# RWKV stage of a hybrid diffusion step, reordered around its serial chains, with the key norm moved into the stage before

## The reference

```python
kkf = heads(kc * k_k)                                    # keys of the RWKV branch
kk = kkf * lax.rsqrt(jnp.sum(kkf * kkf, axis=-1) + 1e-12)     # the key norm
decay = jnp.exp(-jnp.exp(-jax.nn.softplus(-(w0[d] + tanh(wlr) @ w2[d])) - 0.5))
a = jax.nn.sigmoid(a0[d] + alr @ a2[d])
kd = kc * (1 + (a - 1) * k_a)
# per token, per direction, per head:
sa = einsum('bhij,bhj->bhi', s, -kk)
s = s * wt + sa * (kk * a) + vt * kt
y = einsum('bhij,bhj->bhi', s, rt)
```

## Time and profile before

| | us |
|---|---|
| median of 3 runs (2185.05 to 2187.41) | 2186.7 |
| the profiled execution's own time | 2176.87 |
| its span | 2175.1 |
| PE busy, share of the span | 1938.8, 89% |
| stage 3, layer 0 | 455.6 to 761.1 |
| stage 3, layer 1 | 1528.5 to 1800.1 |

### The profile page before, as it was taken

How to read it: one execution, slowest core, us unless ns; L and a number is a source line. 1 busy time by engine, 2 the same in 40 slices (tenths; PEclk the granted TensorE clock), 3 DMA queues, 4 the chain that set the end, 5 groups by cost and what they waited for, 6 DMA issues and landing times.

```text
span 2175.1 us, 35742 instructions
## 1 busy us (share of the span) xinstructions
PE 1938.8 (89%) x15251; PEld 1568.5 (72%) x15251; DVE 1025.5 (47%) x1715; ACT 817.8 (38%) x1310; POOL 296.4 (14%) x550
## 2 busy tenths in 40 slices
PE   6899898967888888999989999989768888899998
PEld 2799445644565588999989975556446668899998
DVE  0326425847463464433333444286656655434332
ACT  1533544253332345333234344333523344533321
POOL 2000000007455000000000000000275520000000
PEclk9999999987989999999999999999889999999999
DMA  7443334301303143443443432433010203344442
GB/s 263 135 120 107 103 97 128 115 25 40 98 2 99 45 164 97 118 134 110 122 133 100 127 99 80 141 102 117 6 44 18 60 7 116 97 136 117 118 120 83
DMA packets 267782, 214.32 MB, mean 99 GB/s; under 512 B 7210, under 2 KB 259401, under 8 KB 267369
## 3 DMA queue, kind: packets, MB, share of 16 engines
q1 hardware_dynamic: 264640, 204.43, 31.1%
q0 software_dynamic: 2736, 7.54, 1.1%
q10 hardware_dynamic: 248, 0.07, 0.0%
HBM read 209.13 MB, written 2.88 MB: 97 GB/s over the span
## 4 chain that ended last, share of the span: by engine, by line
PE 74%; DVE 9%; ACT 8%; POOL 3%; issue 3%; DMA 1%; PEld 1%; PEldq 1%; DVEq 0%; ACTq 0%; POOLq 0%
PE bank L554 11%; PE bank L555 11%; PE bank L556 11%; PE bank L610 8%; PE bank L605 7%; PE bank L930 3%; PE bank L1110 3%; PE bank L1109 3%; PE bank L1108 3%; PE bank L616 3%; PE bank L506 2%; POOL cst L1191 2%; PE bank L794 2%; POOL lora L1189 2%; ACT h L1255 1%
## 5 line engine op out<-in xcount | busy, mean ns | idle before, releaser
L556 PE MATMUL bank<-scr_rounded 128*128 128x384 f32 (+1 forms) x1312 | 443.0, 338 | 0.0
L554 PE MATMUL bank<-scr_rounded 128*128 128x384 f32 x672 | 231.8, 345 | 36.0 <-DVE scr_rounded L1676 34.2
L610 PE MATMUL bank<-h,ring 128*128 128x384 f32 x640 | 240.6, 522 | 20.2 <-ACT gtmp L1238 14.2
L556 PEld LDWEIGHTS bank<-scr_rounded 128*128 128x128 f32 (+1 forms) x1312 | 248.8, 190 | 1.0
L555 PE MATMUL bank<-scr_rounded 128*128 128x384 f32 x672 | 229.5, 342 | 0.0
L1671 DVE TENSOR_TENSOR scr_rounded<-ring,scr_rounded 128x2048 fp32r<-128x2048 f32 (+1 forms) x64 | 136.0, 2126 | 175.9 <-ACT scr_rounded L1246 175.1
L554 PE MATMUL bank<-scr_rounded,gate_rounded 128*128 128x384 f32 (+1 forms) x640 | 214.0, 334 | 4.4 <-DVE scr_rounded L1671 4.4
L555 PE MATMUL bank<-scr_rounded,gate_rounded 128*128 128x384 f32 (+1 forms) x640 | 213.8, 334 | 0.0
L610 PEld LDWEIGHTS bank<-h,ring 128*128 128x128 f32 x640 | 121.9, 200 | 107.6 <-issue 40.0
L605 PE MATMUL bank<-ring,scond 128*2 128x256 f32 x768 | 177.1, 383 | 23.8 <-ACT modrow L1225 8.2
L1671 DVE TENSOR_TENSOR scr_rounded<-ring,gate_rounded 128x2048 fp32r<-128x2048 f32 (+3 forms) x64 | 130.2, 2034 | 104.8 <-ACT gate_rounded L1246 104.3
(11 more groups left out here) (368 smaller groups left out, 3218.1 us busy)
## 6 DMA issues: line engine op xcount, KB each, us to landing
ring<-in_w_in_dram SPq DMA_DIRECT2D x56, 1024.0 KB, 5.3
ring<-in_w_ada_dram SPq DMA_DIRECT2D x48, 1024.0 KB, 5.2
ring<-in_w_ffn_in_dram SPq DMA_DIRECT2D x88, 512.0 KB, 5.1
ring<-in_w_ffn_out_dram SPq DMA_DIRECT2D x32, 704.0 KB, 4.6
ring<-in_w_out_dram SPq DMA_DIRECT2D x8, 1024.0 KB, 5.2
ring<-in_w_po_a_dram SPq DMA_DIRECT2D x4, 1024.0 KB, 6.3
ring<-in_w_po_b_dram SPq DMA_DIRECT2D x4, 1024.0 KB, 5.4
ring<-in_w_po_c_dram SPq DMA_DIRECT2D x4, 1024.0 KB, 5.2
```

Source lines behind the costliest of these rows:

```text
L554: pe.matmul(o, w_hi[:, k, :], right[0][k], start=k == 0, stop=False)
L556: ins = pe.matmul(o, w_lo[:, k, :], right[0][k], start=False, stop=k == nk - 1)
L610: ins = pe.matmul(b[:, 0:T], w[:, k, 128 * (j % 2):128 * (j % 2) + 128], h[:, k, :], start=k == 0, stop=k == KD - 1)
```

## The change

- The squares of the keys and their sums move from stage 3 into stage 2, with their own buffers `kkn`. `unit_keys` for all pairs comes first on DVE in stage 3. `loras(0)` moves ahead of the barrier.
- `reads` (RT) goes right behind W, ahead of FT. The second half of a group's terms is split (`keys`, `terms`), and the two groups of the next pair go between the evictions of the state chain. Before, they stood behind `factors`.
- `grams(n + 1)` goes ahead of `turned(n)`. `ee` gets a third buffer.
- `FILLS` becomes a list for each layer, with more places, and `side_plan(2)` puts its two gates last.

```diff
-        FILLS = ((2, 8, 2, 0), (2, 2, 4, 0), (2, 2, 4, 0), (2, 2, 0, 4))
+        FILLS = ((4, 4, 4, 4, 6, 0, 2, 4, 2, 1, 1, 1, 0, 0, 1, 2, 1, 1, 1, 0, 0, 1, 2, 1, 1, 1, 2, 2, 2, 2, 2, 1, 1, 1),
+                 (4, 4, 4, 4, 4, 0, 2, 4, 0, 1, 1, 1, 0, 0, 1, 1, 1, 1, 1, 0, 0, 1, 1, 1, 1, 1, 2, 2, 2, 0, 0, 1, 1, 1))
...
-                return po[0:4] + ada[0:4] + po[4:8] + [gate_of(1, 0), ada[4], gate_of(1, 1)] + ada[5:8]
+                return po[0:4] + ada[0:4] + po[4:8] + ada[4:8] + [gate_of(1, 0), gate_of(1, 1)]
...
-                fill(4)
+                for hp in range(4):
+                    pe.wait_ge(S["rw_kksq"], told("rw_kksq", l, hp + 1))
+                    pe.wait_ge(*room())
+                    b = item("A", "kkms", l, hp)
+                    pe.matmul(b[:, 0:T], blocks, kkn[hp], start=True, stop=True).then_inc(psum_ready, 1)
+                fill(3)
...
-                    fill(2)
+                    fill(2 if n < 12 else 1)
...
@@ PE, stage 3 @@
+                fill(next(steps))
                 loras(2)
                 grams(0)
+                fill(next(steps))
+                loras(3)
+                fill(next(steps))
                 for n in range(5):
                     if n:
                         merges(n - 1)
                         transitions(n - 1)
+                        fill(next(steps))
                         scan_step(n - 1, 0)
-                        reads(n - 1)
+                        if n < 3:
+                            loras(2 * n + 3)
                         scan_step(n - 1, 1)
-                        fill(1)
+                        fill(next(steps))
                         scan_step(n - 1, 2)
-                        fill(1)
+                        fill(next(steps))
                         outputs(n - 1)
...
@@ ACT, stage 2 @@
+                for hp in range(4):
+                    A(kkn[hp], pc[:, 4 + hp, :], ACT.Square, scale=P(l, "k_k", hp)).then_inc(*tells("rw_kksq"))
                 act.wait_ge(S["gla_abs"], told("gla_abs", l, 1))
...
@@ ACT, stage 3 @@
+                decays(2)
                 for n in range(5):
...
@@ DVE, stage 3 @@
                     if n:
                         inverses(n - 1)
+                        reads(n - 1)
                     if n < 3:
-                        logs(2 * n + 2)
+                        keys(2 * n + 2)
                     if n:
                         transitions(n - 1)
+                    if n < 3:
+                        terms(2 * n + 2)
+                    if n:
                         scan_step(n - 1, 0)
-                        reads(n - 1)
                         scan_step(n - 1, 1)
+                    if n < 3:
+                        logs(2 * n + 3)
+                    if n:
                         scan_step(n - 1, 2)
+                    if n < 3:
+                        keys(2 * n + 3)
+                        terms(2 * n + 3)
                     if n < 4:
                         factors(n)
                         if n < 3:
-                            terms(2 * n + 2)
-                            logs(2 * n + 3)
-                            terms(2 * n + 3)
+                            grams(n + 1)
+                        if n < 2:
+                            logs(2 * n + 4)
                         turned(n)
```

More of the change, by code:

```diff
@@ L830, in loras @@
                         pe.matmul(b[:, 0:T], lora[hr[d], w, 128 * hp:128 * hp + 128], pc[hr[d], src, :], start=True, stop=True).then_inc(psum_ready, 1)
+                pe.wait_ge(S["rw_lora"], told("rw_lora", l, 1))
+                loras(0)
+                finish(l, 2)
+                barrier(pe, "pe", l, 2)
+                side[0] = side_steps(side_plan(l, 3))
                 def grams(n):
@@ L1394, in _ @@
                 A(lg, lg, ACT.Ln, bias=1.0).then_inc(*tells("gla_log"))
+                for hp in range(4):
+                    side_work("kkms", l, hp)
+                    act.wait_ge(psum_ready, filled("kkms", l, hp))
+                    b = bank("kkms", l, hp)
+                    A(kkn[hp], b[:, 0:T], ACT.Ln, bias=eps[:, 1:2], scale=1.0).then_inc(*empties("kkms", l, hp))
                 for cc in range(C):
@@ L1407, in _ @@
                 A(ke[:, 2:4, :], be[:, 2:4, :], ACT.Exp, scale=-1.0 / 16).then_inc(*tells("gla_exps"))
+                act.wait_ge(*last())
+                for hp in range(4):
+                    A(kkn[hp], kkn[hp], ACT.Exp, scale=-0.5).then_inc(*tells("rw_kkr"))
                 for m in range(4):
@@ L1530, in _ @@
                 decays(0)
-                for hp in range(4):
-                    A(kkb[hp], pc[:, 4 + hp, :], ACT.Square, scale=P(l, "k_k", hp)).then_inc(*tells("rw_kksq"))
-                for hp in range(4):
-                    side_work("kkms", l, hp)
-                    act.wait_ge(psum_ready, filled("kkms", l, hp))
-                    b = bank("kkms", l, hp)
-                    A(gate[:, hp, :], b[:, 0:T], ACT.Ln, bias=eps[:, 1:2], scale=1.0).then_inc(*empties("kkms", l, hp))
-                act.wait_ge(*last())
-                for hp in range(4):
-                    A(gate[:, hp, :], gate[:, hp, :], ACT.Exp, scale=-0.5).then_inc(*tells("rw_kkr"))
                 exps(0)
@@ L1570, in _ @@
                         exps(2 * n + 2)
+                        decays(2 * n + 3)
+                        exps(2 * n + 3)
                     if n:
@@ L1574, in _ @@
                         factors(n)
[L1575 to L1577 removed]
+                        if n < 2:
+                            decays(2 * n + 4)
                         turned(n)
@@ L1937, in logs, with keys @@
                     dve.wait_ge(*last())
+                def keys(g):
+                    hp, d = groups[g]
+                    bt, kdd = BT[hp % 2][d], kd0 if d == 0 else sg
+                    side_work("al", l, g)
+                    dve.wait_ge(*emptied("al", l, g))
+                    ts(kdd, aa, P(l, "k_a", hp), oka[:, hp:hp + 1], mult, add).then_inc(*step())
+                    stt(out=bt[:, :, 0, :], in0=c6(kkb[hp]), scalar=-1.0, in1=c6(aa), op0=mult, op1=mult).then_inc(*step())
+                    dve.wait_ge(*last())
+                    tt(kdd, kdd, pc[:, k_ + hp, :], mult).then_inc(*step())
                 def terms(g):
@@ L1955, in terms @@
                     ends = slice(1, 6, 4) if d == 0 else slice(0, 1)
-                    tt(ee[i][d][:, here], es1[:, here], es0[:, after], mult).then_inc(*step())
+                    tt(ee[hp % 3][d][:, here], es1[:, here], es0[:, after], mult).then_inc(*step())
                     dve.wait_ge(*last())
-                    cp(ee[i][d][:, ends], es1[:, ends]).then_inc(*step())
+                    cp(ee[hp % 3][d][:, ends], es1[:, ends]).then_inc(*step())
                     if d == 1:
@@ L2032, in scan_step @@
                             c = scanned(d, 1)[0]
-                            stt(out=hfin[:, 4 * d + hp, :], in0=bank("H", l, n, s, d)[:, 64:128], scalar=ee[i][d][:, c:c + 1], in1=gE[:, d, c, :],
+                            stt(out=hfin[:, 4 * d + hp, :], in0=bank("H", l, n, s, d)[:, 64:128], scalar=ee[n % 3][d][:, c:c + 1], in1=gE[:, d, c, :],
                                 op0=mult, op1=add).then_inc(*empties("H", l, n, s, d))
-                def reads(n):
-                    i = n % 2
-                    for d in range(2):
-                        tt(RTt[:, d, :, :], taken("RT", n, d), ar[i][d][:, :, 1, :], add).then_inc(*empties("RT", l, n, d))
                 def factors(n):
@@ L2085, in unit_keys @@
                     dve.wait_ge(S["rw_kkr"], told("rw_kkr", l, hp + 1))
-                    stt(out=kkb[hp], in0=pc[:, k_ + hp, :], scalar=P(l, "k_k", hp), in1=gate[:, hp, :], op0=mult, op1=mult).then_inc(*step())
+                    stt(out=kkb[hp], in0=pc[:, k_ + hp, :], scalar=P(l, "k_k", hp), in1=kkn[hp], op0=mult, op1=mult).then_inc(*step())
+                for hp in range(4):
+                    unit_keys(hp)
+                dve.wait_ge(*last())
                 logs(0)
-                unit_keys(0)
-                dve.wait_ge(*last())
+                keys(0)
                 terms(0)
                 logs(1)
-                for hp in range(1, 4):
-                    unit_keys(hp)
-                dve.wait_ge(*last())
+                keys(1)
                 terms(1)
@@ L2102, in _ @@
                 begin(0)
+                logs(2)
                 for n in range(5):
```

72 lines of the change are left out of this document (24 added, 48 removed).

## The result

The change makes the kernel slower: 2201.45 us (median of 4 runs) against 2186.19, a ratio of 1.0076 with an interval of 1.0059 to 1.0093. I had forecast 2186 and no change. The profiled execution took 2198.93 us. A repeat of after beside later variants gave 2203.89 and 1.0092 (1.0068 to 1.0116).

What follows compares the result with a forecast made beforehand. PE, busy 89%, was taken as the bound, its idle 236 us as what an order can win. Terms gave -7.7 (layer 0) and +6.8 (layer 1), together -0.9 on 2176.87; with 9.8 to the median, 2186, range 2163 to 2203.

Steps and rivals of the forecast that it cites:

- End of stage 2: Side work and key norm late in stage 2: its closing barrier comes 1.7 us later in each layer.
- the two gates left for `finish`: Tail of stage 2: the second gate waits for ACT to empty the first; 4 steps, 5.6 us, plus a sigmoid.
- The key norm's matmuls lie in PE's idle time: Stage 2: the moved products, 2.6 us on PE, were to fit where PE idles.
- 0.9 stays: Stage 2: squares delay ACT's exponential by 1.5 us; DVE already waited 0.6 longer for side work, so 0.9 is left.
- The start: Stage 3, barrier to first POOL chain: handover at 30.5 us, -4.9 and -4.4; the key norm alone would give 8.5.
- The first chain: Stage 3, first POOL chain: its end is missed; 47.5 us in layer 0 (+7.2), 43.8 in layer 1 (+3.5).
- The key price: DVE's keys, terms and logs for two groups beside POOL's chain: taken as 16.3 us, between 10.6 and 18.0.
- the last quarter meets the chain's short last operations: Reason for pricing DVE's keys, terms and logs at 16.3 us instead of the full 18.0 beside POOL.
- Rival B: DVE's idle time takes the terms in: iterations 1 and 2 fall to about 48 us, kernel 2163; chance 0.25.
- Rival C: DVE's list becomes the bound; PE waits over 5 us for MT and restarts at low clock: 2200 us, chance 0.25.
- Iteration 3 of layer 1: Stage 3: 10 side steps instead of 2, taken out of iterations 1 and 2, arrive here: +10.2 us.
- The base: Profiled execution of before, 2176.87 us, on which the sum was made; the median of three runs is 9.8 above.

## Why the prediction was wrong, point by point

Means of two profiles of each kernel, us, after less before. The spans differ by +18.7 (2197.1 and 2198.5 against 2175.1 and 2183.0), of which -0.7 lies outside stages 2 and 3:

| term | forecast L0, L1 | measured L0, L1 |
|---|---|---|
| stage 2 | +1.7, +1.7 | +9.1, +8.5 |
| start | -4.9, -4.4 | -4.0, -3.7 |
| first chain | +7.2, +3.5 | +5.4, +3.4 |
| iteration 1 | -12.1, -3.1 | -10.6, -0.7 |
| iteration 2 | -4.4, -2.0 | -2.7, -1.8 |
| iteration 3 | +3.6, +10.2 | +4.3, +9.6 |
| iteration 4 | +1.2, +0.9 | +2.5, +0.1 |

**The step that failed is "End of stage 2".** It should have been the whole of stage 2. 14.2 us of the 19.6 that the sum was off are there, and the two kernels that differ only in stage 2 differ by 16 us. Its own piece, the two gates left for `finish`, was right: the tail grew by 1.5 where I had 1.7. Two things were not walked:

- *The scan loop.* The prediction has no term for it, so it stood at nothing, without a reason; 26 side steps stand in it where before there were 28. It grew by 4.5 us in each layer. Which item a step belongs to matters: an odd number of steps ahead of the loop, 7, put modulation columns across two scan steps, and PE waited 4.4 us in the loop instead of 0.8. The side work's old order takes all of it back. One step more, which makes the number even, takes 5.1 from the loop and 3.6 net.
- *"The key norm's matmuls lie in PE's idle time", "0.9 stays".* The 0.9 was right: DVE's operation behind the logarithm starts 11.1 us into the stage instead of 10.25. But the products did not lie in idle time: they run at 342.96 to 345.99, ahead of the side work, and PE's waits come later. And PE, with 3 side steps fewer, waited 3.5 and 4.1 us there instead of 3.0 and 2.6, and what follows ran at the low clock. The transposes and the chunk products ahead of the loop, in before:

```profile
361.92 1.09 PE L506 MATMUL bank<-cst,scr 128*128 128x128 f32 x8 [2.60 <-DVE scr L1845]
362.94 1.97 PE L780 MATMUL bank<-gate,scr 128*64 128x128 f32 x32
```

and in after:

```profile
364.94 1.97 PE L508 MATMUL bank<-cst,scr 128*128 128x128 f32 x8 [4.07 <-DVE scr L1843]
366.84 3.36 PE L787 MATMUL bank<-gate,scr 128*64 128x128 f32 x32
```

That is 2.3 of the 3.0 us. The granted clock of the piece is 0.85, against 1.00. With the side work's old order these two took 1.09 and 1.97 us again, but DVE then waited for side work behind the products, and the piece was as long. I had priced cold starts in stage 3 and nowhere else.

**The start** was right: 31.2 us against 30.5, and the key norm alone gives 8.6 and 7.1 where I said 8.5. The first chain, 45.9 and 45.3 in the first profile for 47.5 and 43.8, too; the terms that the prediction lists for layer 0 add up to 46.9, not 47.5.

**The key price** was too low, and the reasoning right. Keys, terms and logs of an iteration, 26 operations, took 19.6 us beside POOL and 13.7 in before (the earlier trace rows has 18.0 and 10.6 for 25 others). The full price was paid, the upper of my two bounds, which I had moved down by "the last quarter meets the chain's short last operations". The rule of the Trainium skill that the prediction weighed ("SBUF — State Buffer", "Who interferes with whom") says that DVE operations with two inputs in SBUF contend with GpSimd's reads, and the traces agree with it: the same operations took 0.55 us without the chain and 0.93 and 0.96 on average beside it. The price was 3.3 us more an iteration than the 16.3 in the sum, but iterations 1 and 2 exceeded their forecast by only 0.2 to 2.4 us. It is not why the kernel is slower: without the placement it is slower still.

**Rival B** did not come: iterations 1 and 2 never went below 53.6 us in after. **Rival C** gave 2200, near the measured time, by another mechanism. PE's wait for MT was 4.0 us in iteration 1 of layer 0 and 0.8 to 2.0 in the others, below the 4.66 at which I let it decide. Only in the first chain of layer 1 was it longer, 8.7 and 8.6 us, over the 5 us named as C's sign, and that chain took 45.3 and 42.2 us for the forecast 43.8. The right number came for the wrong reason, so it is no support for it, and it is luck that the time lies inside the stated range.

**Iteration 3 of layer 1** was forecast as the largest loss (+10.2, measured +9.6), and the lists show the cause: its steps, moved to gaps, give 8.5 to 10.5 back with the changed stage 2 and 4.5 to 6.6 without.

**The base** was off as well. The profile on which I made the sum had iterations 2 and 3 of layer 1 at a clock that the second profile did not get; I corrected for that by the difference to the median, which was right.

## What to carry to other kernels

Filler work is not a number of steps. Walk every list that it passes through, also in stages which the diff touches only with a 3 for a 4, and look at where each item begins and ends, what it waits for, and who must empty it. Put filler into the waits that the profile shows (here the one ahead of G1, 4 to 9 us each) before a serial chain is reordered: the old order with filled gaps was at least as fast as the new one with its best list. And of a change in four parts, price each part alone: one of them, the key norm, was worth 19 us once its squares and its products stood where no other engine waited behind them.
